# Orders of copies, exponentials and projections in two attentions, and stationary weights in the FFN input projections

## The reference

```python
def swiglu(h, w_in, w_out):
    a, b = jnp.split(h @ w_in, 2, axis=-1)
    return (jax.nn.silu(a) * b) @ w_out
...
for l in range(DEPTH):
    if l == N_A_LAYERS:
        k_sh, v_sh, c_sh = shared_kv(x, kv_norm_g, fox_w_kvf, fox_b_f)
    x = x + 0.5 * swiglu(rms_norm(x, norm_g[l, 0]), ffn_w_in[l, 0], ffn_w_out[l, 0])
    h = rms_norm(x, norm_g[l, 1])
    x = x + (nsa_mixer(h, ...) if l < N_A_LAYERS else fox_mixer(h, ...))
    x = x + 0.5 * swiglu(rms_norm(x, norm_g[l, 2]), ffn_w_in[l, 1], ffn_w_out[l, 1])
return rms_norm(x, final_g)
```

## Time and profile before

| | |
|---|---|
| median of 3 runs | 1064.94 us (1064.58 to 1068.81) |
| the profiled execution | 1067.82 us, of which the span is 1065.8 us |
| PE busy / PEld busy | 1046.3 us (98%) / 870.7 us (82%), 5156 matmuls |
| DVE / ACT / POOL busy | 598.0 us (56%) / 525.9 us (49%) / 73.4 us (7%) |
| chain that ended last | PE 95%, DVE 2%, ACT 1%, issue 1% |
| DMA | 182.45 MB, mean 171 GB/s |

### The profile page before, as it was taken

How to read it: one execution, slowest core, us unless ns; L and a number is a source line. 1 busy time by engine, 2 the same in 40 slices (tenths; PEclk the granted TensorE clock), 3 DMA queues, 4 the chain that set the end, 5 groups by cost and what they waited for, 6 DMA issues and landing times.

```text
span 1065.8 us, 14153 instructions
## 1 busy us (share of the span) xinstructions
PE 1046.3 (98%) x5156; PEld 870.7 (82%) x5156; DVE 598.0 (56%) x833; ACT 525.9 (49%) x692; POOL 73.4 (7%) x108
## 2 busy tenths in 40 slices
PE   8999999999999999999999999999998999999997
PEld 7888888888888888888888888888887888888886
DVE  5545545777475564445567775445565556555444
ACT  7433444656475554433455543443465646334444
POOL 0040000000013000000000390000000000000000
PEclk9999999999899999999999999999999999999999
DMA  7685756457201365555544665555544136555541
GB/s 248 228 228 188 242 180 223 160 178 242 93 2 41 118 198 197 191 167 193 198 156 160 237 197 197 197 177 188 187 158 158 41 108 213 187 185 194 197 158 40
DMA packets 128709, 182.45 MB, mean 171 GB/s; under 512 B 5960, under 2 KB 100272, under 8 KB 128544
## 3 DMA queue, kind: packets, MB, share of 16 engines
q1 hardware_dynamic: 127040, 176.18, 49.8%
q0 software_dynamic: 1456, 5.72, 2.4%
q10 hardware_dynamic: 176, 0.05, 0.0%
HBM read 180.34 MB, written 1.59 MB: 171 GB/s over the span
## 4 chain that ended last, share of the span: by engine, by line
PE 95%; DVE 2%; ACT 1%; issue 1%; DMA 0%; ACTq 0%; DVEq 0%
PE inb L405 15%; PE inb L403 15%; PE inb L404 15%; PE acc L403 13%; PE acc L405 13%; PE acc L404 13%; PE inb L640 2%; PE tb L512 2%; PE acc L613 2%; PE tb L625 2%; PE inb L637 1%; PE tb L592 1%; DVE work L1461 1%; PE acc L397 0%; PE tb L397 0%
## 5 line engine op out<-in xcount | busy, mean ns | idle before, releaser
L1321 DVE TENSOR_TENSOR wlo<-raw,whi 128x2048 fp32r<-128x2048 f32 x108 | 250.1, 2316 | 233.7 <-ACT whi L927 233.7
L927 ACT CAST whi<-raw 128x2048 fp32r<-128x2048 f32 x108 | 206.5, 1912 | 217.3 <-PE acc L405 117.8
L403 PE MATMUL inb<-whi,thi 128*128 128x512 f32 x720 | 281.7, 391 | 0.0
L405 PE MATMUL inb<-whi,tlo 128*128 128x512 f32 x720 | 280.5, 390 | 0.0
L404 PE MATMUL inb<-wlo,thi 128*128 128x512 f32 x720 | 280.2, 389 | 0.0
L405 PEld LDWEIGHTS inb<-whi,tlo 128*128 128x128 f32 x720 | 135.2, 188 | 28.5
L404 PEld LDWEIGHTS inb<-wlo,thi 128*128 128x128 f32 x720 | 135.2, 188 | 27.9
L403 PEld LDWEIGHTS inb<-whi,thi 128*128 128x128 f32 x720 | 135.2, 188 | 27.8
L1304 DVE TENSOR_TENSOR wlo<-raw,whi 128x2048 fp32r<-128x2048 f32 x55 | 128.7, 2344 | 47.1 <-ACT whi L914 46.9
L403 PE MATMUL acc<-whi,ghi 128*128 128x512 f32 x320 | 128.5, 402 | 0.0
L405 PE MATMUL acc<-whi,glo 128*128 128x512 f32 x320 | 125.1, 391 | 0.0
(11 more groups left out here) (231 smaller groups left out, 988.0 us busy)
## 6 DMA issues: line engine op xcount, KB each, us to landing
raw<-in_ffn_w_in SPq DMA_DIRECT2D x174, 512.0 KB, 4.8
raw<-in_ffn_w_out SPq DMA_DIRECT2D x88, 512.0 KB, 4.0
raw<-in_nsa_w_in SPq DMA_DIRECT2D x20, 512.0 KB, 4.2
raw<-in_fox_w_kvf SPq DMA_DIRECT2D x16, 512.0 KB, 4.3
raw<-in_nsa_cmp_w SPq DMA_DIRECT2D x8, 512.0 KB, 4.8
raw<-in_nsa_w_out SPq DMA_DIRECT2D x8, 512.0 KB, 4.5
raw<-in_fox_w_q SPq DMA_DIRECT2D x8, 512.0 KB, 4.4
raw<-in_fox_w_out SPq DMA_DIRECT2D x8, 512.0 KB, 4.6
```

Source lines behind the costliest of these rows:

```text
L403: pe.matmul(o, lh, rh, start=start, stop=False, skip_group_check=True)
L405: return pe.matmul(o, ll, rh, start=False, stop=stop, skip_group_check=True)
L927: act.copy(whi[u % RING][:, :], raw[u % RING][:, :]).then_inc(s_hi, 1)
L1321: dve.tensor_tensor(wlo[u % RING][:, :], raw[u % RING][:, :], whi[u % RING][:, :].bitcast(F32), ALU.subtract).then_inc(s_lo, 1)
```

## The change

In the FFN chunks after the first, the sides of the input projection are exchanged: a 128x128 block of weights is stationary and the activations move (`unit_turned`). For this `thi` and `tlo` become two halves of one tensor `th`, so that one matmul with `whi` stationary moves 512 columns (256 of the high, 256 of the low part) and a second with `wlo` stationary moves 256 columns (high part). Four blocks of columns fill the four banks `inb` and `tb`: two for a, two for b. The result has hidden columns on partitions and tokens along the row, so it needs no turn. DVE adds each bank's two halves (`summed`, a tensor_reduce), multiplies a by a row of `rstd` (`silu_input`), ACT applies silu to both a blocks at once, DVE multiplies by b (`hidden_product`), and the split into `ghi`, `glo` is taken from SBUF. The factor `rstd` on the b side moves into the residual add (`rstd_hf`). The row of `rstd` is made once per FFN by two small products on PE (`rstd_rows`) and a copy on DVE. The first chunk keeps the old form, turned into `acc[2]`. In the last chunk the turn for the following stage stands ahead of the last 12 matmuls.

In the attentions: on ACT, `exps(2)` stands behind the two `q_half` copies in NSA, and likewise `exps(18)` in FoX; FoX's `hi(U_FOXQ + 5)` stands ahead of `exps(16)`. On PE, `scores(18)` stands ahead of the wait `copied(11)`, and `project_first` moves, in both mixers, from ahead of the last `turn_probs` to behind the following `values`, next to `turn_o(2)`.

```diff
-thi = sb("thi", [P, KT, SEQ], F32R)
-tlo = sb("tlo", [P, KT, SEQ], F32R)
+th = sb("th", [P, KT, 2, SEQ], F32R)
...
+thi, tlo = th[:, :, 0, :], th[:, :, 1, :]
...
+mbanks = [inb[0], inb[1], tb[0], tb[1]]
...
-    def hidden_turn(need, tiles=range(NT)):
+    def hidden_turn(need):
         pe.wait_ge(s_g, need)
         for k in range(2):
-            for t in tiles:
-                mm = pe.transpose(tb[0][:, k * SEQ + t * P:k * SEQ + (t + 1) * P],
+            for t in range(NT):
+                mm = pe.transpose(acc[2][:, k * SEQ + t * P:k * SEQ + (t + 1) * P],
                                   gg[:, t, k * P:(k + 1) * P], ident[:, :])
         mm.then_inc(s_gt, 1)
+    def rstd_rows(name):
+        pe.wait_ge(s_rstd, NORMS.index(name) + 1)
+        for t in range(NT):
+            mm = pe.matmul(acc[3][:, t * P:(t + 1) * P], rstd[:, t:t + 1].broadcast_to([P, P]),
+                           ident[:, :], start=True, stop=True)
+        mm.then_inc(s_rrow, 1)
+    def unit_turned(slot, half, need, banks_free=None):
+        pe.wait_ge(s_lo, need)
+        if banks_free is not None:
+            pe.wait_ge(s_sum, banks_free)
+        for m in range(4):
+            for k in range(4):
+                kk = 4 * half + k
+                col = slice(k * CW + m * P, k * CW + (m + 1) * P)
+                pe.matmul(mbanks[m][:, :], whi[slot][:, col], th[:, kk].rearrange("p x n -> p (x n)"),
+                          start=kk == 0, stop=False, skip_group_check=True)
+                mm = pe.matmul(mbanks[m][:, 0:SEQ], wlo[slot][:, col], th[:, kk, 0, :],
+                               start=False, stop=kk == KT - 1, skip_group_check=True)
+            if half == 1 and m < 3:
+                mm.then_inc(s_in, 1)
+        mm.then_inc(s_used, 1)
     def ffn(f, following=None):
-        b, n0, h0 = U_FFN[f], NJ * f, (NJ + 1) * f
+        b, h0, c0 = U_FFN[f], NJ * f, 4 * (NJ - 1) * f
         if f == 0:
             first_chunk_of_all(acc[0:2])
             pe.wait_ge(s_setup, 2)
         else:
             first_chunk(b, acc[0:2], f"ffn{f}", [(s_nat_a, 9), (s_nat_d, 9)] if f == 2 else None)
-        unit_in((b + 2) % RING, 0, inb, b + 3)
-        hidden_turn(2 * (n0 + 1))
-        unit_in((b + 3) % RING, 1, inb, b + 4)
+        unit_turned((b + 2) % RING, 0, b + 3)
+        hidden_turn((NJ + 1) * f + 2)
+        rstd_rows("kv" if f == 2 else f"ffn{f}")
+        unit_turned((b + 3) % RING, 1, b + 4)
         pe.wait_ge(s_lo, b + 5)
-        pe.wait_ge(s_glo, 1 + h0)
+        pe.wait_ge(s_glo, h0 + 1)
+        pe.wait_ge(s_rc, f + 1)
         slot = (b + 4) % RING
         out_part(slot, 0, 0, True)
         out_part(slot, 0, 1)
         out_part(slot, 1, 0, True)
-        hidden_turn(2 * (n0 + 2))
         out_part(slot, 1, 1).then_inc(s_used, 1)
         with pe.Fori(2, NJ - 1) as j:
-            for half in range(2):
-                u = b + 2 + half
-                unit_in(u % RING, half, inb, 3 * (j - 1) + u + 1)
+            unit_turned((b + 2) % RING, 0, 3 * (j - 1) + b + 3, 4 * (j - 1) + c0)
+            unit_turned((b + 3) % RING, 1, 3 * (j - 1) + b + 4)
             pe.wait_ge(s_lo, 3 * (j - 1) + b + 5)
             pe.wait_ge(s_glo, j + h0)
-            slot = (b + 4) % RING
             out_part(slot, 0, 0)
             out_part(slot, 0, 1)
             out_part(slot, 1, 0)
-            hidden_turn(2 * j + 2 * n0 + 2)
             out_part(slot, 1, 1).then_inc(s_used, 1)
         u = b + 3 * (NJ - 1) - 1
-        for t in range(NT):
-            for half in range(2):
-                pe.wait_ge(s_lo, u + half + 1)
-                mm = rows4((u + half) % RING, half, t, inb[t][:, :])
-                if t == NT - 1:
-                    mm.then_inc(s_used, 1)
-                    if half == 0:
-                        pe.wait_ge(s_glo, h0 + NJ - 1)
-                        hidden_turn(2 * (n0 + NJ) - 1, [0])
-            if t == 0:
-                mm.then_inc(s_in0, 1)
+        unit_turned(u % RING, 0, u + 1, 4 * (NJ - 2) + c0)
+        unit_turned((u + 1) % RING, 1, u + 2)
         pe.wait_ge(s_lo, u + 3)
+        pe.wait_ge(s_glo, h0 + NJ - 1)
         out_part((u + 2) % RING, 0, 0)
         out_part((u + 2) % RING, 0, 1)
+        out_part((u + 2) % RING, 1, 0)
         pe.wait_ge(s_lo, u + 4)
         pe.wait_ge(s_glo, h0 + NJ)
         out_last((u + 3) % RING, 0)
-        hidden_turn(2 * (n0 + NJ), [1])
-        out_part((u + 2) % RING, 1, 0)
-        pe.wait_ge(s_glo, h0 + NJ + 1)
+        out_part((u + 2) % RING, 1, 1).then_inc(s_used, 1)
         if following:
             turn(following, 0)
-        out_part((u + 2) % RING, 1, 1).then_inc(s_used, 1)
         out_last((u + 3) % RING, 1)
...
+    def last_items():
+        project_first(U_NSA_OUT, 0)
+        turn_o(2, 0)
     items(0, nsa_keys, nsa_values, 16,
-          {15: lambda: project_first(U_NSA_OUT, 0)},
+          {},
           {4: cmp_turn, 6: lambda: cmp_values(0), 7: lambda: cmp_values(1),
            8: lambda: cmp_values(2), 9: lambda: cmp_values(3), 11: lambda: turn_o(0, 0),
-           13: lambda: turn_o(1, 0), 15: lambda: turn_o(2, 0)})
+           13: lambda: turn_o(1, 0), 15: last_items})
...
     turn_probs(16, 16)
+    scores(18, 2, 2)
     copied(11)
-    scores(18, 2, 2)
     values(16, 16, fox_values(0))
     pair_round(18, xn, 2)
     pair_round(19, xn, 3)
+    def last_items():
+        project_first(U_FOX_OUT, 4)
+        turn_o(2, 4)
     items(16, lambda i: i, fox_values, 8,
-          {1: lambda: rounds_copied(20), 7: lambda: project_first(U_FOX_OUT, 4)},
-          {3: lambda: turn_o(0, 4), 5: lambda: turn_o(1, 4), 7: lambda: turn_o(2, 4)})
+          {1: lambda: rounds_copied(20)},
+          {3: lambda: turn_o(0, 4), 5: lambda: turn_o(1, 4), 7: last_items})
...
+    def silu_turned(n):
+        act.wait_ge(s_ar, n)
+        act.activation(sa[:, :, :], sa[:, :, :], ACT.Silu).then_inc(s_silu, 1)
+    def hidden_turned_hi(n):
         act.wait_ge(s_gt, n)
...
+        act.copy(ghi[:, :, :].rearrange("p k n -> p (k n)"), acc[2][:, :]).then_inc(s_ghi, 1)
+    def hidden_hi(n, dst):
+        act.wait_ge(s_g, n)
+        act.copy(dst.rearrange("p k n -> p (k n)"),
+                 gg[:, :, :].rearrange("p k n -> p (k n)")).then_inc(s_ghi, 1)
     def ffn(f):
-        b, h0 = U_FFN[f], (NJ + 1) * f
-        act.wait_ge(s_in0, 2 * f + 1)
+        b, a0, g0 = U_FFN[f], (NJ - 1) * f, (NJ + 1) * f
+        act.wait_ge(s_in0, f + 1)
         silu_tile(0, acc)
         act.wait_ge(s_used, b + 2)
         silu_tile(1, acc)
         if f:
             hi(b + 3)
         hi(b + 4)
+        hidden_turned_hi(f + 1)
         with act.Fori(1, NJ - 1) as j:
-            act.wait_ge(s_used, 3 * (j - 1) + b + 2)
-            hidden_hi(j + h0)
             hi_loop(b + 5, j)
-            silu(3 * (j - 1) + b + 4)
+            silu_turned(j + a0)
             hi_loop(b + 6, j)
+            act.wait_ge(s_used, 3 * (j - 1) + b + 5)
+            hidden_hi(j + g0 + 2, ghi[:, :, :])
             hi_loop(b + 7, j)
...
         hi(b + FFN_UNITS - 1)
-        act.wait_ge(s_used, b + FFN_UNITS - 2)
-        silu_tile(1)
+        silu_turned(a0 + NJ - 1)
+        hidden_hi(g0 + NJ + 1, ghi_last)
         hi(b + FFN_UNITS)
-        hidden_last_hi(h0 + NJ + 1, 1)
...
     exps(1)
-    exps(2)
     q_half(10, 2)
     q_half(11, 3)
+    exps(2)
...
+    hi(U_FOXQ + 5)
     exps(16)
     exps(17)
-    hi(U_FOXQ + 5)
     chunk_q(inb[0], 1, U_FOXQ + 4)
     pt_copy(16)
-    exps(18)
     q_half(18, 2)
     q_half(19, 3)
+    exps(18)
...
+        dve.tensor_scalar(rstd_hf[:, :], rstd[:, :], 0.5, None, ALU.mult)
...
-    def hidden_tile(n, t, banks=inb):
+    def hidden_tile(n, t):
         dve.wait_ge(s_silu, n + 1)
...
+        dve.tensor_tensor(gg[:, t, :], acc[t][:, FC:2 * FC], sa[:, t, :], ALU.mult).then_inc(s_g, 1)
+    def hidden_turned_lo(n):
         dve.wait_ge(s_ghi, n)
-        dve.tensor_tensor(glo[:, :, :].rearrange("p k n -> p (k n)"), tb[0][:, :],
+        dve.tensor_tensor(glo[:, :, :].rearrange("p k n -> p (k n)"), acc[2][:, :],
                           ghi[:, :, :].rearrange("p k n -> p (k n)").bitcast(F32),
                           ALU.subtract).then_inc(s_glo, 1)
-    def hidden_last_lo(n, t):
+    def summed(m):
+        dst = (sa if m < 2 else gg)[:, m % 2, :]
+        dve.tensor_reduce(dst, mbanks[m][:, :].rearrange("p (x n) -> p n x", x=2), AX.X,
+                          ALU.add).then_inc(s_sum, 1)
+    def silu_input(n):
+        dve.wait_ge(s_sum, n)
+        dve.tensor_tensor(sa[:, :, :], sa[:, :, :], rstd_row[:, :].unsqueeze(1).broadcast_to([P, 2, SEQ]),
+                          ALU.mult).then_inc(s_ar, 1)
+    def hidden_product(n, summed_n):
+        dve.wait_ge(s_sum, summed_n)
+        dve.wait_ge(s_silu, n)
+        dve.tensor_tensor(gg[:, :, :], gg[:, :, :], sa[:, :, :], ALU.mult).then_inc(s_g, 1)
+    def hidden_lo(n, hi_part, lo_part):
         dve.wait_ge(s_ghi, n)
...
```

(68 more changed lines are left out.)

20 lines of the change are left out of this document (removed).

## The result

The changed kernel takes 1056.65 us (median of 6 runs, 1055.28 to 1058.4) against 1064.99: a ratio of 0.9917, 95% interval 0.9903 to 0.993. It is faster by 8.3 us where 23.5 were forecast. The profiled execution took 1058.4 us with a span of 1056.7, 9.1 less than before.

A forecast was written before the change was run, and what follows sets the result against it. PE's own work was taken to bound the FFNs, most of the span, with waits and low clock in the attentions. FFNs -7.2 and attentions 16.3 less gave -23.5 us: 1041.4, range 1036 to 1047, chance 0.50.

The forecast's parts named there:

- mixed units: FFN chunks: input units of 16 matmuls of 512 columns and 16 of 256 instead of 24 of 512; 5.1 us more.
- rows of `rstd`: FFNs: two products with the identity per FFN, 0.61 us for two, cost PE 2.4 us in all.
- FFN ends: Three FFN ends with a following stage: PE waits 0.3 and 1.1 us, with drains 1.5 each, 4.5 us; bounds 0 and 3.
- NSA: NSA attention: first items gain 4.4 us (1.1 if the clock falls), `project_first` moved behind `values` gains 3.4 us.
- FoX: FoX attention: wait at `copied(11)` and its low clock go, 5.3 us; `project_first` moved gains 3.2 us.
- I take 0.1173, the row with the same type and width: FFN input units: step of a 256-column matmul, taken from NSA's compression, 15 steps in 1.76 us.
- those eight scores: Attention scores with 128 stationary columns, four 256 and four 128 wide: 0.92 us, at most 0.115 each, cited for 0.1173.
- Rival (e): FFN chunks: load of 128 stationary columns not hidden under 256 moving, step 0.188, 91 us more, 1132; chance 0.06.
- 0.9 is nearer to the first: NSA's first items: PE's gap of 0.9 us, nearer to 0.60 (kept full clock) than 1.49 (lost it), keeps the clock; 3.3 us.
- rival (c): FFN sums: operands 256 elements apart make a sum take twice 0.69, 8.3 us at four ends, 1049.7; chance 0.07.
- Rival (a): New waits in NSA and at three FFN ends also drop the clock, 8.4 us in all, 1049.8; chance 0.18.
- Rival (d): Attentions: waits are only exchanged, so only the FFNs' 7.2 us remain, 1057.7; chance 0.08.

The follow-up runs named there:

- the split: Changed kernel with each 512-wide matmul of `unit_turned` split into two of 256, the same stationary block loaded again: 1063.91 us.
- the order by sixteens: Changed kernel with each unit's sixteen wide matmuls ahead of its sixteen narrow ones, reversed in the second unit, and `cmp_scores` split: 1050.24 us, ratio 0.9853.

## Why the prediction was wrong, step by step

| term | forecast | measured |
|---|---|---|
| turns removed | -19.2 | -19.2: no transpose is left in the loops |
| mixed units | +5.1 | +16.3: 80 x (11.29 / 2 - 5.441) |
| output behind them | 0 | +2.5: 40 x (5.503 - 5.441) |
| rows of `rstd` | +2.4 | some +1.6: 0.82 us more ahead of each FFN's first output, 0.41 of it two mixed units |
| FFN ends | +4.5 | +2.2: three pauses 0.7 longer, the turn's drain included |
| NSA | -7.8 | -4.6, with the attention edits alone |
| FoX | -8.5 | -8.8, with the attention edits alone |
| sum | -23.5 | -10.0; the spans give -9.1 |

Of the 0.9 between the last two, 0.4 is the longer wait ahead of FFN 2, which has no row here.

**The step that failed** is "I take 0.1173, the row with the same type and width", and the sum 0.2267 + 0.1173 built on it. 11.2 of the 15.2 us that are missing are this term, and the 2.5 behind it have the same cause. It failed twice. That row had 60 stationary columns; with 128 the step is 0.120 (the split), 3.5 us in 1280 steps. And the price of a step among its own kind doesn't hold by turns: 6 ns a pair more, 7.7 us, shown by the order by sixteens, where the same matmuls cost 0.347 a pair. Nor did support 0.1173: half of those eight scores move 128 columns, so at most 0.115 is a mean over both widths and says little of a step of 256. Rival (e) had the right resource, a load of 128 columns, but not the size: its floor is 0.113 where (e) put the busy time's 0.188, and the narrow matmul's share of a pair, 0.353 - 0.227 = 0.126, doesn't reach (e)'s point of decision at 0.136. The step of the earlier trace rows looked safe because its load's busy time was longer than the step; but busy time was no measure of the cover that a load needs, 0.113 where 0.188 were recorded.

**NSA's first items:** the wait shrank to 0.84 as forecast (0.9), but "0.9 is nearer to the first" failed: the clock fell, 3.3 us not gained. The forecast went by the length of the wait, and that can't have decided here: before and after, the clock fell 0.3 us into the wait, sooner than the 0.60 that had kept it, and 1.8 and 0.55 us ahead of the wait's end. The rest of NSA came as forecast: of the 4.6, 1.1 arises ahead of the last items (the shorter wait, forecast 1.1) and 3.6 from there on (`project_first`, forecast 3.4).

**FoX** was right, mechanism and size, 8.8 for 8.5, and so was `project_first` in both.

**FFN ends:** the wait is for `wlo`, as forecast, but PE stands 0.7 us longer instead of 1.5. The chain of waits shows it: ACT's copy, its `lo`, tile 0's residual, ACT's squares, the turned halves, tile 1's residual, the next `lo`, PE:

```profile
188.20 1.92 ACT whi L942
...
190.14 2.29 DVE wlo L1325
192.43 1.33 DVE xs L1466 x2
...
196.00 2.16 DVE th L1360 x8
198.16 1.32 DVE xs L1466 x2
199.47 2.21 DVE wlo L1325
...
201.82 0.47 PE inb L411
```

The order is the forecast's, and it ran ahead of it from the start: the last quarter's sum ended 1.4 us after the last chunk's input, not 1.8, and the `lo` that PE wants 16.1 after it, not 16.7. The forecast's first wait of 0.3 didn't come at all.

**Right as well:** DVE's load and layout (a sum takes 0.685 us, forecast 0.69), no wait in the loop on the sums or `glo`; so rival (c) is out. Rival (a) was right in one of its four places. Rival (d) came nearest in time, 1057.7 for 1056.65, by luck: its waits didn't move elsewhere, and its 7.2 us from the FFNs didn't come.

**Open:** what the 6 ns by turns are made of. They showed only where both matmuls have 128 stationary columns and the widths differ. A load's lack of cover alone doesn't explain them, since with 320 columns moving an excess stayed (how large is not shown, as no run has 320 among its own kind). Open as well is what decides NSA's clock, in the same kernel from one execution to the next.

## What to carry to other kernels

Price a matmul from a row with the same stationary columns and the same neighbours, not the same width alone: two steps measured each among its own kind don't add up when they alternate. When a change replaces work by more and shorter pieces on the engine that bounds, measure one chunk of the new mix before counting on the sum, and try the order that keeps equal widths together. Split a change with two independent halves first: here one half gave all the gain. And don't settle a question of the granted clock on one trace of each kernel: read the mean of every execution.
